# Laying out SBUF anew in a two-block fp32 kernel: where the matmuls' operands lie

## The reference

```python
# first block, DEPTH = 2 layers
h = rms_norm(x, g_mix_pre);  u = h @ w_in                    # 1024 -> 3200 columns
mix = concat(chunk_attention(q, k, v), conv_module(cu), retention(rq, rk, rv, rg))
x = x + rms_norm(mix @ w_out, g_mix_post)
f = square(relu(rms_norm(x, g_mlp_pre) @ w_up)) @ w_down      # 1024 -> 4096 -> 1024
x = x + rms_norm(f, g_mlp_post)

# second block, one layer
q, k, v, u, gates = split(rmsnorm(h) @ w_in_2)
attn_branch = rmsnorm(diff_attention(rope(q), rope(k), v)) @ w_attn_proj
g = gelu(s5_scan(u)); ssm_branch = (g * sigmoid(g @ w_glu + b_glu)) @ w_ssm_proj
h = h + (g_attn * attn_branch + g_ssm * ssm_branch) @ w_out
gate, val = split(causal_dwconv(rmsnorm(h) @ w_up))           # 1024 -> 2 x 2816
h = h + (silu(gate) * val) @ w_down                           # 2816 -> 1024
```

## Time and profile before

| | |
|---|---|
| time, median of 3 runs | 2129.18 us (2128.6 to 2130.15) |
| profiled execution, first to last instruction | 2128.8 us |
| PE busy | 2081.8 us, 98% |
| PE weight loads busy | 1660.9 us, 78% |
| DVE, ACT, POOL busy | 1050.8, 877.0, 922.1 us (49, 41, 43%) |
| DMA | 202.29 MB, mean 95 GB/s |
| matmuls | 10168 |

### The profile page before, as it was taken

One profiled execution on the slowest core, in us unless ns is written; L12 is line 12 of the kernel. 1 busy time (PEld: TensorE's weight loads), 2 busy tenths in 40 slices (PEclk: granted clock), 3 DMA queues, 4 the chain that ended last, 5 costly groups with the idle time before them and its releaser, 6 DMA issues.

```text
span 2128.8 us, 27453 instructions
## 1 busy us (share of the span) xinstructions
PE 2081.8 (98%) x10168; PEld 1660.9 (78%) x10168; DVE 1050.8 (49%) x1725; ACT 877.0 (41%) x1221; POOL 922.1 (43%) x306
## 2 busy tenths in 40 slices
PE   8999999999999999999999998999999999999999
PEld 6875788888888775888888886777776787888887
DVE  4866252222237664332222248886488534464555
ACT  5355462222334445542322252265477434333332
POOL 5523444444355423545665457224222344444442
PEclk9999999999999999999999999999999999999999
DMA  4532222322323431233323224232211232332232
GB/s 158 172 114 66 73 80 92 98 87 98 99 89 124 143 90 43 76 99 99 99 81 97 99 77 154 83 89 92 80 60 60 99 99 80 99 97 87 92 99 79
DMA packets 120050, 202.29 MB, mean 95 GB/s; under 512 B 6544, under 2 KB 51856, under 8 KB 119696
## 3 DMA queue, kind: packets, MB, share of 16 engines
q1 hardware_dynamic: 112992, 189.12, 27.2%
q10 hardware_dynamic: 6960, 11.88, 1.9%
HBM read 189.44 MB, written 8.12 MB: 93 GB/s over the span
## 4 chain that ended last, share of the span: by engine, by line
PE 75%; issue 15%; DVE 5%; POOL 3%; ACT 0%; DMA 0%; ACTq 0%; DVEq 0%; POOLq 0%
PE bank L718 63%; PE bank L820 5%; POOL w_lo L523 3%; PE bank L829 1%; PE bank L796 1%; PE bank L772 1%; PE bank L847 1%; PE bank L887 1%; PE bank L875 1%; PE bank L1017 0%; PE bank L781 0%; DVE w L2395 0%; DVE pr L2056 0%; PE bank L913 0%; DMA tmul<-in_tmul 0%
## 5 line engine op out<-in xcount | busy, mean ns | idle before, releaser
L523 POOL TENSOR_TENSOR w_lo<-raw,w_hi 128x2048 fp32r<-128x2048 f32 (+1 forms) x167 | 741.8, 4442 | 1109.6 <-ACT w_hi L1389 1109.6
L718 PE MATMUL bank<-act_hi,w_hi 128*128 128x512 f32 x1424 | 567.7, 399 | 3.6 <-DVE hid L2604 2.5
L1389 ACT ACTIVATE w_hi<-raw 128x2048 fp32r<-128x2048 f32 (+1 forms) x170 | 314.1, 1848 | 598.0 <-PE bank L718 539.9
L718 PE MATMUL bank<-act_hi,w_lo 128*128 128x512 f32 x1424 | 556.8, 391 | 0.0
L718 PE MATMUL bank<-act_lo,w_hi 128*128 128x512 f32 x1424 | 556.4, 391 | 0.0
L718 PEld LDWEIGHTS bank<-act_hi,w_hi 128*128 128x128 f32 x1424 | 268.7, 189 | 73.0 <-issue 13.0
L718 PEld LDWEIGHTS bank<-act_hi,w_lo 128*128 128x128 f32 x1424 | 268.2, 188 | 57.7
L718 PEld LDWEIGHTS bank<-act_lo,w_hi 128*128 128x128 f32 x1424 | 268.6, 189 | 55.0 <-issue 1.4
L718 PE MATMUL bank<-h_hi,w_hi 128*128 128x512 f32 x704 | 277.6, 394 | 0.3 <-DVE x L2569 0.3
L718 PE MATMUL bank<-h_hi,w_lo 128*128 128x512 f32 x704 | 277.4, 394 | 0.0
L718 PE MATMUL bank<-h_lo,w_hi 128*128 128x512 f32 x704 | 277.4, 394 | 0.0
(11 more groups left out here) (371 smaller groups left out, 2714.2 us busy)
## 6 DMA issues: line engine op xcount, KB each, us to landing
raw<-in_w_up SPq DMA_DIRECT2D x32, 1024.0 KB, 5.5
raw<-in_w_down SPq DMA_DIRECT2D x32, 1024.0 KB, 5.0
raw<-in_w_in SPq DMA_DIRECT2D x26, 1024.0 KB, 5.1
raw<-in_w_up SPq DMA_DIRECT2D x44, 512.0 KB, 4.5
raw<-in_w_in SPq DMA_DIRECT2D x28, 768.0 KB, 4.6
raw<-in_w_out SPq DMA_DIRECT2D x12, 1024.0 KB, 5.0
raw<-in_w_down SPq DMA_DIRECT2D x22, 512.0 KB, 4.2
raw<-in_w_attn_proj SPq DMA_DIRECT2D x4, 1024.0 KB, 5.1
```

The lines of the kernel that those rows point to most:

```text
L523: pool.tensor_tensor(m.w_lo[slot][:, 0:n], m.raw[slot][:, 0:n], m.w_hi[slot][:, 0:n].bitcast(F32), ALU.subtract).then_inc(s["split_ready"], 1)
L718: mm = pe.matmul(o, ll if i == 2 else lh, rl if i == 1 else rh, start=first and n == 0, stop=last and n == len(steps) - 1)
L1389: act.activation(m.w_hi[slot][:, 0:n], m.raw[slot][:, 0:n], ACT.Copy).then_inc(s["w_hi"], 1)
```

## The change

The order of the tensors in the partition is changed, and nothing else in the work: every engine has the same instructions, in the same order, with the same semaphores and shapes. Three small things go with it. `h_hi` and `h_lo` go to the start of the arena and `f` and `both` make room: `f` moves from 16 to 40 KB into it, the first use of `both` gets its own place (`both_first`), and the GELU output of the second block, which used `h_hi[0]` and `h_lo[0]`, gets its own pair (`u_hi`, `u_lo`, called `gelu` in the profile) at 40 KB into the arena.

```diff
     m = Memory()
+    m.act_hi = put("act_hi", [P, KD, T], F32R)
+    m.act_lo = put("act_lo", [P, KD, T], F32R)
+    arena = (top[0] + 63) // 64 * 64
+    top[0] = arena + ARENA_KB * 1024
+    m.w_hi = [put(f"w_hi{i}", [P, UNIT], F32R) for i in range(2)]
+    m.w_lo = [put(f"w_lo{i}", [P, UNIT], F32R) for i in range(2)]
     m.x = put("x", [P, KD, T])
     x_at = top[0] - 4 * NT * D
-    m.act_hi = put("act_hi", [P, KD, T], F32R)
-    m.act_lo = put("act_lo", [P, KD, T], F32R)
     m.raw = [put(f"raw{i}", [P, UNIT]) for i in range(2)]
-    m.w_hi = [put(f"w_hi{i}", [P, UNIT], F32R) for i in range(2)]
-    m.w_lo = [put(f"w_lo{i}", [P, UNIT], F32R) for i in range(2)]
     m.cmat = put("cmat", [P, 5, P])
...
     late_at = top[0]
     top[0] += 4 * 4 * T
-    arena = (top[0] + 63) // 64 * 64
...
-    m.f = ar("f", [P, KD, T], 16)
+    m.f = ar("f", [P, KD, T], 40)
...
-    m.h_hi = [ar(f"h_hi{i}", [P, 4, T], 40 + 16 * i, F32R) for i in range(2)]
-    m.h_lo = [ar(f"h_lo{i}", [P, 4, T], 48 + 16 * i, F32R) for i in range(2)]
+    m.h_hi = [ar(f"h_hi{i}", [P, 4, T], 16 * i, F32R) for i in range(2)]
+    m.h_lo = [ar(f"h_lo{i}", [P, 4, T], 8 + 16 * i, F32R) for i in range(2)]
+    m.both_first = ar("both_first", [P, T], 56)
...
+    m.u_hi, m.u_lo = (ar(f"gelu{i}", [P, 4, T], 40 + 8 * i, F32R) for i in range(2))
...
-    feature_major(4, 1, ah=m.h_hi[0], al=m.h_lo[0], to=GLU_BANKS)
+    feature_major(4, 1, ah=m.u_hi, al=m.u_lo, to=GLU_BANKS)
```

More of the change, by code:

```diff
@@ L92 @@
 TURN_A, TURN_B = 8, N_SUB // 8
+ARENA_KB = 95
 LN_EXP, SQRT = "natural_log_exp_and_others", "sqrt_and_others"
@@ L320, in memory @@
     top[0] += 4 * 4 * T
-    arena = (top[0] + 63) // 64 * 64
+    assert top[0] <= nc.sbuf_usable_end, top[0]
     def ar(name, shape, kb, dt=F32):
+        assert kb * 1024 + 4 * int(np.prod(shape[1:])) <= ARENA_KB * 1024, name
         return put(name, shape, dt, at=arena + int(kb * 1024))
@@ L596, in turns @@
         wide = lambda x: x[:].rearrange("p (s a b) -> p s a b", s=4, a=TURN_A)
-        sin, cos, both = wide(m.sin_n[b]), wide(m.cos_n[b]), wide(m.both)
+        sin, cos, both = wide(m.sin_n[b]), wide(m.cos_n[b]), wide(m.both if b else m.both_first)
         of = slice(4 * b, 4 * b + 4)
@@ L1796, in functions @@
             for b in range(4):
-                copy_hi(in_chunks(m.h_hi[0][:, b, :]), in_time(m.uT[:, b, :]), "h_hi")
+                copy_hi(in_chunks(m.u_hi[:, b, :]), in_time(m.uT[:, b, :]), "h_hi")
             act.preload_act_table_set(LN_EXP)
@@ L2480, in arithmetic @@
             for b in range(4):
-                low(in_chunks(m.h_lo[0][:, b, :]), in_time(m.uT[:, b, :]), in_chunks(m.h_hi[0][:, b, :]), "h_hi", "h_lo")
+                low(in_chunks(m.u_lo[:, b, :]), in_time(m.uT[:, b, :]), in_chunks(m.u_hi[:, b, :]), "h_hi", "h_lo")
         for g in range(2):
```

## The result

| | before | changed |
|---|---|---|
| time, median of 6 runs each | 2128.89 us (2125.39 to 2130.92) | 2111.72 us (2109.41 to 2116.72) |
| ratio, with its 95% interval | 1 | 0.9931 (0.9920 to 0.9943), 14.7 us less |
| span of the profiled execution | 2128.8 us | 2108.7 us |

The account below looks back on a forecast made before the run. PE was taken to bound the kernel, busy 98% of the span at 2.4 GHz. Terms of -16.2 + 3.7 + 0.3 = -12.2 us took 2128.8 to 2116.6, called 2117 us; range 2110 to 2131.

Parts of the forecast that it names:

- Term 1: h, a, sum and gated, as moving operands, go below 128 KB: 2496 matmuls each 6.5 ns shorter, 16.2 us gained.
- Term 2: Weights as moving operands go above 128 KB: 576 matmuls each lose 6.5 ns, 3.7 us lost.
- Is it the place in SBUF?: Step on PE's matmuls: moving operands below 97 KB pay about 13.5 ns each, those above 128 KB about 20.
- the second: Rival: the slower pace belongs to something else those four moving operands share; time stays 2129 us; chance 0.08.
- Term 3: Weights as stationary operands go above 128 KB, for 4848 + 2496 matmuls: taken as zero, bounds 6.5 ns each either way.
- the stationary operand costs the same: Rival: a matmul pays the longer price if either operand is above 128 KB; +35 us, 2164 us; chance 0.17.
- Term 5: Given back in the second MLP's last group, where PE waits for DVE: 48 matmuls x 6.5 ns, 0.3 us.
- The place does nothing: Rival: something else shared by h, a, sum and gated sets the slower pace; time 2129 us; chance 0.08.
- Apart is better than together: Rival: weights above, activations below would save a further 6.5 ns on 7344 matmuls, 48 us: 2069 us; chance 0.05.

Follow-up runs that it names:

- e2: Changed kernel with arena and the weights behind it 64 bytes further up, act left in place: 2137.75 us, ratio to before 1.0057.
- e1: Kernel before with only the arena start rounded to 128 bytes, 64 bytes further up, all tensors in their old regions: 2113.72 us, ratio to before 0.9939.
- e3: Changed kernel with the weights and everything behind them 64 bytes further up, act and arena left: 2153.76 us, ratio to before 1.0132.
- e10: Changed kernel with VectorE emptying banks 6 and 7 before, not after, multiplying into hid2 in the second MLP: 2109.56 us, ratio to before 0.9929.
- e4: Changed kernel with all its tensors 896 bytes up, so act, arena and weights start at multiples of 1024 bytes: 2113.29 us, ratio to before 0.9938.
- e5: Changed kernel with everything 64 bytes up, so act, arena and weights all start 64 bytes off a multiple of 128: 2110.79 us, ratio to before 0.9929.
- e9: Changed kernel with both weight parts 256 bytes up, act and arena left: ratio to before 0.9943.
- e6: Changed kernel with both weight parts 32 bytes up, act and arena left: ratio to before 1.0117.
- e7: Changed kernel with both weight parts 128 bytes up, act and arena left: ratio to before 1.0102.
- e11: Changed kernel with both weight parts 448 bytes up, act and arena left: ratio to before 0.9998.
- e8: Changed kernel with only w_lo 64 bytes up, w_hi left: ratio to before 1.0056.
- e12: Changed kernel with w_hi 64 bytes off, w_lo on the same start as act and h, the two swapped in memory: ratio to before 1.0081.

## Why the prediction was right, and where it was wrong

**The size of the gain.** Term 1, 2496 matmuls times 6.5 ns, 16.2 us: confirmed in size, not in its reason. The measured difference is 6.67 ns (22.40 less 21.76 over 96), 16.6 us. sum and gated got it too, so the doubt about them was idle.

**The cause was wrong, and that the change worked at all was luck.** The place was to explain the price; the low bits of the starts do. The new layout happens to put the arena right behind act, whose end lies 128 bytes past a multiple of 256, and the weights 95 KB further on, which is a multiple of 256 too. Had the arena come out 64 bytes further on, the same move would have lost 0.6% (e2) and not gained 0.7%.

**Term 2 failed.** 3.7 us were to be lost by the weights as moving operands above 128 KB. They lost nothing. The step that failed stands in "Is it the place in SBUF?": *every moving operand below 97 KB is fast and every one above 128 KB slow*. The rows said that, for the tensors there were; I had looked at their regions in KB and not at their low bits, where the same tensors fall in the same two classes. The question whether a third quantity goes with the place was put to the PSUM bank and to the neighbours, not to the alignment. None of the three rivals named it; the second ("something else that h, a, sum and gated share") left room for it, but took it that the change would then do nothing.

**Term 3.** Zero for the stationary operand's place was right: the weights at 128 to 160 KB are as good as at 65 to 97 (changed kernel against e1). But the stationary operand has its part in the price, by its low bits: moved by 64 bytes it costs 42 us (e3). The first rival, "the stationary operand costs the same", would have been near the truth for a change that moved the weights to an unequal start.

**Term 5 was too small.** 0.3 us given back was for the last group alone. The eleven down groups of the second MLP have 528 matmuls, which at 6.67 ns would be 3.5 us; they became 1.1 us shorter and so gave back 2.4. VectorE empties banks 6 and 7 later than PE's new pace wants them. The earlier trace rows was the wrong place to look; the earlier trace rows was about ScalarE and GpSimd, and I had no row on VectorE's cover. e10 shows it.

**The sum again.** -16.6 (2496 x 6.67), 0 for the weights moving, +2.4 given back: -14.2 us, where the traces have 14.5 from the first weights-moving matmul on and the runs 14.7 (12.1 to 17.0). The forecast of -12.2 holds two errors with opposite signs, 3.7 us too much lost in term 2 and 2.1 too little given back in term 5. That it came near is in part luck too; the measured 2111.72 us lies in the stated range of 2110 to 2131, and just below the 2112 to 2120 that the bounds of the terms gave.

**The rivals.** "The stationary operand costs the same" (2164 us) did not happen with this layout. "The place does nothing" is true as a statement on the place (e1), and wrong as a forecast of the time, since the change does something beside it. "Apart is better than together" is refuted: activations and weights in different halves (changed kernel) and in the same one (e1) have the same 226.7 ns. The Trainium skill's "SBUF — State Buffer", section "SBUF: two separate sides", says that PE never waits on anyone, and speaks there of what engines do to each other. What these runs show is another thing: a price of up to 6.7 ns that goes by the starts of the two operands of PE's own matmuls. Whether it arises where they are read no run shows. The N/2.4 + 2.5 ns of the Trainium skill's "TensorE: Matmul & The Clock Gate", section "Back-to-back issue gap", is given there for an isolated matmul and not for a stream with weight loads, as this one is; the prediction set it against the wrong case, and the 226.7 to 233.3 ns measured here neither confirm nor refute it.

## What to carry to other kernels

In a stream of fp32r matmuls with one weight load each, give the moving and the stationary operand the same start modulo 256 bytes. Here that is a change of one line in an allocator that rounds to 64. It is worth 0.6% against the kernel before, and 2% between the worst and the best layout. When a difference goes with a set of tensors, list every property of their addresses before naming one, and look for a tensor that would change its class under the explanation alone: here the weights as moving operand. A pace that improves by 3% uses up slack of that size on the engines that clear the banks.

## What the runs showed of the hardware

- fp32r matmuls of 512 columns with a 128-column weight load each follow each other at 226.7 to 226.9 ns at the granted 2.4 GHz when the starts agree modulo 256 bytes (changed kernel, e1, e4, e5, e9), and at 232.4 to 233.3 when the moving one is 32, 64 or 128 bytes behind (e6, e3, e7). In 2.4 GHz cycles 226.7 ns are 512 + 32 and 233.3 are 512 + 48. With the moving operand 64 bytes ahead the pace is 228.9 to 229.1 in some stretches and 233.3 in others (e11, e2, e3).
- With one stationary operand of three unequal (e8), or two (e12), a triple of 512 columns takes 693.3 ns; in other stretches of e12 it takes 700.
- Matmuls of 384 columns follow each other at 173.5 ns, and notice less: 173.4 in e3, 176.0 in e7.
- act moving in short bursts between the small float32 matmuls pays about half. In e2, act is unequal in 4848 matmuls, which at 6.67 ns would be 32 us. From the 400th matmul on, the 3432 in stretches of 48 and more take 21.9 us more than in the changed kernel (6.4 ns each), the 1176 in bursts of 6 to 24 take 3.6 us more (3.1 ns each). All in all e2 takes 22.8 us more there, since the small matmuls in between come out 2.4 us shorter and the rest 0.3.
- What the remaining 32 cycles are was not found. A common start of 0, 128 or 192 modulo 256 makes no difference to them.
